# Trunk kernel on one core: who sums the two accumulators, in which order the first loads are requested, and when one weight panel is split

## The chip, the cores and the metric

One core of a Trainium2 chip runs the whole program. The metric is device time in microseconds (us), the median of several executions. The engines are TensorE (PE in the profile, its weight loads PEld), VectorE (DVE), ScalarE (ACT), GpSimd (POOL) and SyncE (SP), which here only requests transfers between HBM and the on-chip memory (SBUF).

## The reference, cut to what matters

Two layers of one trunk work on 256 context tokens and 512 latent tokens of width 1024, all in float32. The second layer drops the context tokens behind its keys and values, so most of its work is on 512 tokens.

```
for i in range(2):
    mod = silu(c) @ w_mod[i] + b_mod[i]           # six vectors per stream: sh1, sc1, gt1, sh2, sc2, gt2
    h = rmsnorm(x, g_mix[i]) * (1 + sc1) + sh1
    cq, ckv, kr, u, qs, ks, vs, gates = split(h @ w_in[i])
    y = merge(latent_attention(cq, ckv, kr), pooled(u), windowed_attention(qs, ks, vs), gates) @ w_out[i]
    x = x + gt1 * y
    f = rmsnorm(x, g_ffn[i]) * (1 + sc2) + sh2
    x = x + gt2 * (routed_experts(f, top 8 of 64) + shared_expert(f))
out = rmsnorm(x_latent, g_final)
```

## The kernel before, in words

**Jobs.** `make_plan` writes one list of jobs. TensorE runs all of them in that order. ScalarE and VectorE walk the same list, each doing its share (an eviction of PSUM, or extra work hung on the job). PSUM is divided into a few buffers used in rotation; `filled` counts jobs that TensorE has finished, `drained` counts evictions. The list begins with `cvec` (turns the two conditioning vectors), `vec 0` and `vec 1` (turn the small per-layer vectors of layer 0 and of layer 1: biases, gains), and then for panels 0 to 3 of the modulation of layer 0 the pair `modr` (16 matmuls on a 2 MB panel of `w_mod`, L933) and `mod` (8 small matmuls, L938). With panel 3 the scales are complete, and the eight `h` jobs turn the normalised tokens and apply scale and shift. Everything else of the layer follows from `h`.

**Loads at the start.** SP requests transfers in the order of its program (L642 to L724): constants, the conditioning vectors, `load_vectors(0)` (six small transfers), the tokens `ctx` (1 MB, L655) and `x` (2 MB, L656), modulation panel 0, `load_vectors(1)` (L650 again), modulation panels 1, 2 and 3, masks and tables. Weight panels go into a ring of three slots of 2 MB: panel n may be requested once the last job that reads panel n - 3 is filled (`load_panel`, L706). So modulation panel 3 is requested behind job `mod 0 0`. When the tokens have landed, ScalarE takes their sums of squares (six, L1237) ahead of its eviction of `modr 0 0`; VectorE then scales them (six, L1617) ahead of its part of `mod 0 0`, and behind its part of `vec 1`.

**Splitting of weights.** Some projections are computed from float32 operands split into a high and a low part: three matmuls each time (L832, L833, L834, in `project3`). ScalarE copies the high part of a piece (512 columns of the panel, `piece_high`), VectorE subtracts it from the piece (L1843, `piece_low`). The projection `u` of the pooled branch needs all eight of its pieces, numbers 12 to 19: `weights2` waits for `piece_low` 20. The order of jobs around it is `ks`, `vs`, `ksp`, `qs 0`, `qs 1`, `qsp 0`, `qs 2`, `qsp 1`, `qs 3`, `qsp 2`, `u 0`, `qsp 3`, `u 1` to `u 3`, and then the windowed attention. `qs` is a projection of 48 matmuls in layer 0 and 24 in layer 1, and `qsp` a small one (L1044) for the rotary part. `split_now` hangs the pieces on jobs: ScalarE splits behind its eviction of `qs n`, VectorE behind its work for `qsp n` (three instructions at L1443 to L1446 and two subtractions at L1689). Before, n is 1 for pieces 12 to 15 and 2 for pieces 16 to 19. The panel itself is requested when `vs` is filled.

**Behind the loop over experts.** The routed and shared results are gathered in HBM in two accumulators, since blocks of rows are added alternately to one and the other. When the loop of a layer is over, SP requests for each tile of 128 tokens both parts (512 KB each, L796). GpSimd adds them (L1990, semaphore `summed`), VectorE multiplies by gt2 (L1596) and adds the result to the tokens (L1597), ScalarE takes the sum of squares, and both work out the factor of the next norm (L1462, L1463 on VectorE). Layer 0 has six tiles and goes on to the `h` jobs of layer 1. Layer 1 has four tiles, each of which VectorE scales (L1590) and SP stores.

Of the kernel before, what the change touches and what calls it, by code (L numbers as in the profile page):

```python
# [13 lines left out]
ALU, ACT, AX = mybir.AluOpType, mybir.ActivationFunctionType, mybir.AxisListType  # L14

P = 128
# [3 lines left out]
NT, CT = TOK // P, CTX // P  # L20
# [34 lines left out]
def active(l):  # L55

    return list(range(NT)) if l < DEPTH - 1 else list(range(CT, NT))
# [239 lines left out]
def build(nc, x, c, ctx, c_ctx, w_mod, b_mod, g_mix, g_ffn, w_in, g_mla_q, g_mla_kv, w_mla_uq, w_mla_ukv, w_pool,  # L297
# [10 lines left out]
    with ExitStack() as stack:  # L308
# [3 lines left out]
        def sem(name):  # L312
            return stack.enter_context(nc.semaphore(name))
# [72 lines left out]
        XT = XA[:].rearrange("p (t d) -> p t d", t=NT)  # L386
# [62 lines left out]
        comb = [w[:, 2048 * i:2048 * i + 2048].rearrange("p (a n) -> p a n", a=2) for w in WSL[0:2] for i in range(3)]  # L449
# [14 lines left out]
        s_x, s_xs, s_xr = sem("s_x"), sem("s_xs"), sem("s_xr")  # L464
        s_csm, s_css = sem("s_csm"), sem("s_css")
        ssq_ready, var_ready, rstd_ready, xn_ready = sem("ssq_ready"), sem("var_ready"), sem("rstd_ready"), sem("xn_ready")
        pre_ssq, pre_var, pre_rstd, summed = sem("pre_ssq"), sem("pre_var"), sem("pre_rstd"), sem("summed")
        rms_rec, rms_sqrt, cn_ready = sem("rms_rec"), sem("rms_sqrt"), sem("cn_ready")
        roped, rope_copied = sem("roped"), sem("rope_copied")
        max_ready, exp_ready, rden_ready = sem("max_ready"), sem("exp_ready"), sem("rden_ready")  # L470
# [13 lines left out]
        s_comb, combined, s_out = [sem(f"s_comb{i}") for i in range(NT)], sem("combined"), sem("s_out")  # L484
# [17 lines left out]
        def after(eng, *name):  # L502

            j = names[name]
            eng.wait_ge(drained[j.drain], j.count)
# [11 lines left out]
        def attn(l, br, i):  # L517

            t, h = active(l)[i // HEADS], i % HEADS
            if br == "m":  # L520
                return t, h, 0, [(0, 0, 512), (512, 512, 256)] if t >= CT else [(0, 0, CTX)]
            if t < CT:
                return t, h, 512, [(512, 0, CTX)]
            a, b = max(CT, t - 1), min(NT - 1, t + 1)
            n = (b - a + 1) * P
            return t, h, 512 - n, [(512 - n, a * P, n), (512, 0, CTX)]
# [14 lines left out]
        def key_tiles(l, br, i):  # L541

            return [k // P + j for _, k, n in attn(l, br, i)[3] for j in range(n // P)]
# [17 lines left out]
        def norm_no(l, i):  # L561
            return [0, NT, 1 + NT + len(active(1))][l] + i + 1
# [45 lines left out]
        def split_now(kind, a):  # L608

            if kind == "S" and a[1] == "m" and 18 <= a[2] < 30:  # L610
                return [a[2] - 18]
            if kind in ("qs", "qsp"):
                return {1: [12, 13, 14, 15], 2: [16, 17, 18, 19]}.get(a[1], [])
            return []

        def gate_panel(l, n2, b):

            return DK // 2 * b + n2
# [4 lines left out]
        def gate_no(n2, b, cc):  # L623
            return DK * b + 2 * n2 + cc
# [16 lines left out]
        def _(sp):  # L641
# [4 lines left out]
            def load_vectors(l):  # L646
                at = 0
                for v in (b_mod, g_mix, g_ffn, pool_scale, g_mla_q, g_mla_kv):
                    rows = v.shape[1] // P
                    sp.dma_start(layer_vecs[l][at:at + rows, :], v[l].rearrange("(k p) -> k p", p=P)).then_inc(s_vecs[l], 16)  # L650
                    at += rows
                assert at == NVEC

            load_vectors(0)
            sp.dma_start(XT[:, 0:CT, :], ctx[0].rearrange("(t p) d -> p t d", p=P)).then_inc(s_x, 16)  # L655
            sp.dma_start(XT[:, CT:NT, :], x[0].rearrange("(t p) d -> p t d", p=P)).then_inc(s_x, 16)  # L656
            def kpn(w, a, b):
                return w[:, a:b].rearrange("(k p) n -> p k n", p=P)

# [38 lines left out]
            def load_panel(n):  # L698
                key, _ = panels[n]
                if n >= RING:  # L700

                    sp.wait_ge(filled, panels[n - RING][1].fill)
                for at, ks, src in panel_parts(key):
                    w = src.shape[2]
                    dst = ring[:, SLOT * (n % RING) + at:SLOT * (n % RING) + at + ks * w]
                    sp.dma_start(dst.rearrange("p (k n) -> p k n", k=ks), src).then_inc(s_panel[n % RING], 16)  # L706
# [3 lines left out]
            def load_until(key):  # L710
                while done[0] <= panel_no[key]:
                    load_panel(done[0])
                    done[0] += 1

            load_until(("mod", 0, 0))
            for l in range(1, DEPTH):
                load_vectors(l)
            load_until(("mod", 0, 3))
# [3 lines left out]
            for l in range(DEPTH):  # L722
                A = active(l)
# [443 lines left out]
        def _(act):  # L1167
# [60 lines left out]
            for job in act_jobs:  # L1228
# [192 lines left out]
                for i in split_now(kind, a) if kind != "qsp" else ():  # L1421
                    key, at, high = split_piece(l, i)
                    loaded(act, key)
                    if i == 4:

                        act.wait_ge(filled, panels[panel_no["qs_high", l] - RING][1].fill)
                    elif i == 12:
                        act.wait_ge(filled, names["yT", l, "m", NT - 1].fill)
                    copy(high, ring[:, at:at + 512]).then_inc(piece_high, 1)
# [3 lines left out]
        def _(dve):  # L1433
            vec = nc.vector
            tt, ts, stt = vec.tensor_tensor, vec.tensor_scalar, vec.scalar_tensor_tensor

            def link(ins):
                step("dve", dve, ins)
# [21 lines left out]
            def inv_mean(out_, in_, n):  # L1460

                link(ts(out_, in_, 1.0 / n, EPS, ALU.mult, ALU.add))  # L1462
                return vec.reciprocal(out_, out_)  # L1463
# [109 lines left out]
            def combine(l):  # L1573

                A = active(l)
                for s in range(2 if l < DEPTH - 1 else 1):
                    after(dve, "bc", l, "gt2", s)

                def finish(i):

                    t = A[i]
                    if l < DEPTH - 1:
                        dve.wait_ge(pre_ssq, NT * l + i + 1)
                        inv_mean(ssq[:, t:t + 1], ssq[:, t:t + 1], D).then_inc(pre_var, 1)
                        return
                    dve.wait_ge(ssq_ready, norm_no(l + 1, i))
                    inv_mean(ssq[:, t:t + 1], ssq[:, t:t + 1], D).then_inc(var_ready, 1)
                    dve.wait_ge(s_gfin, 16)
                    dve.wait_ge(rstd_ready, norm_no(l + 1, i))
                    stt(XT[:, t, :], XT[:, t, :], rstd[:, t:t + 1], BC["A2", 0], ALU.mult, ALU.mult)\  # L1590
                        .then_inc(fin_ready, 1)

                for i, t in enumerate(A):
                    a = comb[i]
                    dve.wait_ge(summed, i + 1 + (NT if l else 0))
                    link(tt(a[:, 0, :], a[:, 0, :], BC["gt2", 0 if t >= CT else 1], ALU.mult))  # L1596
                    tt(XT[:, t, :], XT[:, t, :], a[:, 0, :], ALU.add).then_inc(combined, 1)  # L1597
                    if i:
                        finish(i - 1)
                finish(len(A) - 1)  # L1600
# [6 lines left out]
            for job in jobs:  # L1607
                kind, a, ps = job.kind, job.args, slot[job.slot] if job.drain else None
                mine = job.drain == "dve"
                l = a[0] if a else 0  # L1610
# [23 lines left out]
                elif kind == "mod":  # L1634
# [6 lines left out]
                    if a[1] in (3, 11):  # L1641
# [4 lines left out]
                        i, g, m = (0, V_GM, 1) if a[1] == 3 else (1, V_GF, 4)  # L1646
# [12 lines left out]
                elif kind in ("rq", "rk"):  # L1659
                    i = int(kind == "rk")  # L1660
# [44 lines left out]
                elif kind == "S":  # L1705
                    _, br, i = a
                    t, h, at, parts = attn(l, br, i)
# [26 lines left out]
                elif kind == "PV":  # L1734
                    _, br, i = a
                    t, h = attn(l, br, i)[:2]
# [8 lines left out]
                elif kind == "yT":  # L1745
                    _, br, t = a
# [9 lines left out]
                elif kind == "b":  # L1756
                    _, n2, b, cc = a
                    i = gate_no(n2, b, cc)
# [9 lines left out]
                    i = gate_panel(*a[:3])  # L1768
# [4 lines left out]
                elif kind == "o":  # L1773
                    t = a[1]
# [65 lines left out]
                for i in split_now("S" if kind == "T" else kind, a) if kind == "qsp" or kind == "T" and a[3] == 0 else ():  # L1840
                    _, at, high = split_piece(l, i)
                    dve.wait_ge(piece_high, PIECES * l + i + 1)
                    tt(ring_r[:, at:at + 512], ring[:, at:at + 512], high, ALU.subtract).then_inc(piece_low, 1)  # L1843
# [3 lines left out]
        def _(pool):  # L1847
            gp = nc.gpsimd
# [22 lines left out]
            for l in range(DEPTH):  # L1871
                A, sl = active(l), L[l]
# [5 lines left out]
                for g in range(4):  # L1878
# [3 lines left out]
                    src, a, b = 0, lo + 1, hi  # L1882
                    for d in (1, 2, 4)[:g]:
                        a, b = a + d, b - d
# [99 lines left out]
                pool.sem_inc(turns, 1)  # L1984
                loop_end(pool)

                for i, t in enumerate(A):
                    a = comb[i]
                    pool.wait_ge(s_comb[i], 32 * (l + 1))
                    gp.tensor_tensor(a[:, 0, :], a[:, 0, :], a[:, 1, :], ALU.add).then_inc(summed, 1)  # L1990


def constants():

# [67 lines left out]
```

## Time and profile before

| | |
|---|---|
| median of 3 runs | 3455.66 us (3450.21 to 3458.8) |
| profiled execution | 3455.1 us, its span 3453.3 us |
| PE busy | 3139.9 us (91%) |
| DVE busy | 1740.1 us (50%) |
| ACT busy | 1369.1 us (40%) |
| POOL busy | 709.5 us (21%) |
| mean of HBM traffic | 222 GB/s |

The span is the time between the first and the last instruction of the profiled execution. A busy share is an average over very different stages. All times in rows are us from the start of the span, unless marked ns. The granted clock is 1.00 at 2.4 GHz and 0.50 at 1.2 GHz.

### The profile page before, as it was taken

The page shows a single profiled execution, that of the slowest core. Times are in us where ns is not written, and L with a number is a line of the kernel's source. Part 1 is how long each engine was busy: PE and PEld are TensorE (multiplying, and loading weights), DVE is VectorE, ACT ScalarE, POOL GpSimd, SP SyncE. Part 2 cuts the span into 40 slices and gives each one's busy share as a digit, 9 for nine tenths or more (in the row PEclk, how much of TensorE's full clock was granted, in tenths as well). Part 3 has the DMA queues.
Part 4 walks back from the last instruction along what each step waited for, and adds up shares of the span by engine and source line. Part 5 has one row for each costly group of instructions (what it writes and reads, how often), then busy time and mean ns, then how long its engine had stood idle before and what let it go on. Part 6 is the DMA issues. An engine that isn't in the chain of part 4 may idle for free.

```text
span 3453.3 us, 49036 instructions
## 1 busy us (share of the span) xinstructions
PE 3139.9 (91%) x14864; PEld 2221.4 (64%) x14864; DVE 1740.1 (50%) x2560; ACT 1369.1 (40%) x1977; POOL 709.5 (21%) x767
## 2 busy tenths in 40 slices
PE   6999999999997999999999499999996899999994
PEld 3468877899545666666666346776863666666663
DVE  1354371222354666666666336362333666666665
ACT  2253251221224555555554235252212555555552
POOL 0000310000062333323332200020003332333332
PEclk9999999999999999999999799999998899999997
DMA  6420113333328999999998510113232999999993
GB/s 225 120 86 7 52 44 104 128 128 134 138 67 323 343 355 343 348 351 354 351 345 278 167 50 1 34 56 92 92 118 98 338 345 334 338 343 336 326 329 129
DMA packets 223714, 703.54 MB, mean 204 GB/s; under 512 B 55650, under 2 KB 104196, under 8 KB 169428
## 3 DMA queue, kind: packets, MB, share of 16 engines
q1 hardware_dynamic: 176356, 601.80, 47.0%
q0 software_dynamic: 47248, 100.21, 10.9%
q8 instruction: 77, 1.26, 0.2%
q14 instruction: 33, 0.27, 0.0%
HBM read 669.89 MB, written 98.31 MB: 222 GB/s over the span
## 4 chain that ended last, share of the span: by engine, by line
PE 63%; DMA 19%; DVE 6%; issue 6%; ACT 3%; SPq 2%; another core or an unknown queue 1%; DVEq 1%; POOLq 0%; POOL 0%; ACTq 0%
DMA ring<-in_w_exp_up 9%; PE ps L825 7%; PE ps L906 6%; PE ps L832 6%; PE ps L833 6%; PE ps L834 6%; DMA region_v<-in_w_exp_up 5%; PE ps L854 5%; PE ps L1104 4%; PE ps L877 4%; DMA region_k<-in_w_exp_up 4%; PE ps L879 4%; PE ps L878 4%; PE ps L1009 3%; PE ps L1030 3%
## 5 line engine op out<-in xcount | busy, mean ns | idle before, releaser
L1956 POOL DMA_INDIRECT acc<-region_q,idx_out x141 | 226.3, 1605 | 922.3 <-DVE region_q L1569 815.3
L877 PE MATMUL ps<-region_h_split,region_q_split 128*128 128x512 f32 x846 | 349.8, 413 | 69.1 <-DVE region_q_split L1529 33.7
L1535 DVE TENSOR_TENSOR ring_split<-ring,region_h_split 128x1024 fp32r<-128x1024 f32 x210 | 246.8, 1222 | 252.5 <-ACT region_h_split L1171 242.4
L854 PEld LDWEIGHTS ps<-con,region_c 128*128 128x128 f32 x1686 | 220.2, 167 | 147.1 <-DVE region_c L1542 73.6
L1171 ACT ACTIVATE region_h_split<-ring 128x1024 fp32r<-128x1024 f32 x210 | 210.1, 1052 | 240.8 <-DMA ring<-in_w_exp_up 201.3
L834 PE MATMUL ps<-region_x_split,ring_split 128*128 128x384 f32 (+2 forms) x800 | 283.0, 354 | 0.0
L854 PE MATMUL ps<-con,region_c 128*128 128x128 f32 x1686 | 258.0, 281 | 26.2 <-DVE region_c L1542 18.0
L906 PE MATMUL ps<-ring,region_c 128*128 128x512 f32 x560 | 252.0, 593 | 1.0 <-DVE region_c L1547 1.0
L1171 ACT ACTIVATE region_q<-ps 128x512 f32<-128x512 f32 (+1 forms) x163 | 106.8, 655 | 351.2 <-PE ps L906 233.9
L877 PEld LDWEIGHTS ps<-region_h_split,region_q_split 128*128 128x128 f32 x846 | 162.0, 192 | 117.6 <-issue 88.0
L878 PE MATMUL ps<-ring_split,region_q_split 128*128 128x512 f32 x560 | 219.9, 393 | 0.0
L1349 ACT ACTIVATE region_c<-ps 128x768 f32<-128x768 f32 (+1 forms) x48 | 33.8, 704 | 410.1 <-PE ps L834 410.1
L1535 DVE TENSOR_TENSOR region_k_split<-region_k,region_h_split 128x1024 fp32r<-128x1024 f32 x108 | 127.0, 1222 | 137.5 <-ACT region_h_split L1171 126.5
L1535 DVE TENSOR_TENSOR region_v_split<-region_v,region_h_split 128x1024 fp32r<-128x1024 f32 x105 | 123.3, 1221 | 126.7 <-ACT region_h_split L1171 122.0
L1904 POOL DMA_DIRECT2D h_rows<-region_c x10 | 5.7, 572 | 818.3 <-DVE region_c L1793 818.3
L879 PE MATMUL ps<-region_h_split,region_c_split 128*128 128x512 f32 x426 | 168.9, 397 | 0.0
L906 PEld LDWEIGHTS ps<-ring,region_c 128*128 128x128 f32 x560 | 101.2, 190 | 101.8 <-issue 101.6
L879 PE MATMUL ps<-region_h_split,region_q_split 128*128 128x512 f32 x420 | 166.6, 397 | 0.0
L832 PE MATMUL ps<-region_x_split,region_q_split 128*128 128x384 f32 (+1 forms) x432 | 157.9, 365 | 7.5 <-DVE ring_split L1457 4.6
L1171 ACT ACTIVATE region_h_split<-region_k 128x1024 fp32r<-128x1024 f32 x108 | 108.4, 1053 | 129.0 <-DMA region_k<-in_w_exp_up 110.9
L834 PEld LDWEIGHTS ps<-region_x_split,ring_split 128*128 128x128 f32 x800 | 151.1, 189 | 11.7
L1171 ACT ACTIVATE region_h_split<-region_v 128x1024 fp32r<-128x1024 f32 x105 | 104.7, 1051 | 125.9 <-DMA region_v<-in_w_exp_up 103.5
(315 smaller groups left out, 6909.9 us busy)
## 6 DMA issues: line engine op xcount, KB each, us to landing
ring<-in_w_exp_gate SPq DMA_DIRECT2D x70, 1024.0 KB
ring<-in_w_exp_up SPq DMA_DIRECT2D x70, 1024.0 KB
ring<-in_w_exp_down SPq DMA_DIRECT2D x70, 1024.0 KB
ring<-in_w_mod SPq DMA_DIRECT2D x24, 2048.0 KB, 8.0
region_k<-in_w_exp_gate SPq DMA_DIRECT2D x36, 1024.0 KB
region_k<-in_w_exp_up SPq DMA_DIRECT2D x36, 1024.0 KB
region_k<-in_w_exp_down SPq DMA_DIRECT2D x36, 1024.0 KB
region_v<-in_w_exp_gate SPq DMA_DIRECT2D x35, 1024.0 KB
```

The lines of the kernel that those rows point to most:

```text
L825: last = mm(ps[0:rows, at:at + n], weight[k], src[k][:, tok:tok + n], start=k == 0, stop=k == len(weight) - 1)
L832: mm(o, wh, xh, start=k == 0, stop=False)
L833: mm(o, wh, xl, start=False, stop=False)
L834: last = mm(o, wl, xh, start=False, stop=k == len(stationary) - 1)
L854: last = nc.tensor.transpose(ps[0:t.shape[1], at:at + t.shape[0]], t, ident[0:t.shape[0], 0:t.shape[0]])
L877: mm(m_gu[s], xT_hi[s][:, k, :], high, start=k == 0, stop=False)
L878: mm(m_gu[s], xT_hi[s][:, k, :], low, start=False, stop=False)
L879: last = mm(m_gu[s], xT_lo[s][:, k, :], high, start=False, stop=k == DK - 1)
L906: last = mm(m_y[:, 512 * side:512 * side + 512], hTb[:, 1 - s, cc * P:cc * P + P], wdn[before][:, cc, 512 * side:512 * side + 512], start= ...
L1171: return A_(o, i, ACT.Copy)
L1535: tt(wgu_lo[w][:, :, 2 * c:2 * c + 2, :], wgu[w][:, :, 2 * c:2 * c + 2, :], wgu_hi[c], ALU.subtract).then_inc(sl["w_lo"], 1)
L1956: pool.indirect_dma_start(ACC[s], bass.IndirectOffsetOnAxis(ap=idx_out[:, s:s + 1], axis=0), yb[:, s, :], None, bounds_check=TOK - 1, oob_ ...
```

## The change

Three edits. VectorE takes over the sum of the two accumulators, waiting for the loads itself; the loop over tiles on GpSimd and its semaphore are gone. SP requests modulation panel 0 ahead of the tokens, and panel 1 ahead of the vectors of layer 1. Pieces 12 to 15 and 16 to 19 are split one job sooner, behind `qs 0` and `qs 1` on ScalarE and behind `qsp 0` and `qsp 1` on VectorE.

```diff
@@ split_now
             if kind in ("qs", "qsp"):
-                return {1: [12, 13, 14, 15], 2: [16, 17, 18, 19]}.get(a[1], [])
+                return {0: [12, 13, 14, 15], 1: [16, 17, 18, 19]}.get(a[1], [])
@@ SyncE
             load_vectors(0)
-            sp.dma_start(XT[:, 0:CT, :], ctx[0].rearrange("(t p) d -> p t d", p=P)).then_inc(s_x, 16)
-            sp.dma_start(XT[:, CT:NT, :], x[0].rearrange("(t p) d -> p t d", p=P)).then_inc(s_x, 16)
...
             load_until(("mod", 0, 0))
+            sp.dma_start(XT[:, 0:CT, :], ctx[0].rearrange("(t p) d -> p t d", p=P)).then_inc(s_x, 16)
+            sp.dma_start(XT[:, CT:NT, :], x[0].rearrange("(t p) d -> p t d", p=P)).then_inc(s_x, 16)
+            load_until(("mod", 0, 1))
             for l in range(1, DEPTH):
                 load_vectors(l)
             load_until(("mod", 0, 3))
@@ VectorE, combine
                 for i, t in enumerate(A):
                     a = comb[i]
-                    dve.wait_ge(summed, i + 1 + (NT if l else 0))
+                    dve.wait_ge(s_comb[i], 32 * (l + 1))
+                    link(tt(a[:, 0, :], a[:, 0, :], a[:, 1, :], ALU.add))
                     link(tt(a[:, 0, :], a[:, 0, :], BC["gt2", 0 if t >= CT else 1], ALU.mult))
                     tt(XT[:, t, :], XT[:, t, :], a[:, 0, :], ALU.add).then_inc(combined, 1)
@@ GpSimd, behind the loop
-                for i, t in enumerate(A):
-                    a = comb[i]
-                    pool.wait_ge(s_comb[i], 32 * (l + 1))
-                    gp.tensor_tensor(a[:, 0, :], a[:, 0, :], a[:, 1, :], ALU.add).then_inc(summed, 1)
```

## Rows read from the trace of the kernel before

**Rows 1.** TensorE's waits, 318 to 410 us and 2150 to 2230: total, times, longest.
```profile
PE ps L832 <- DVE ring_split L1843: 7.6, 1, 7.6
PE ps L832 <- DVE ring_split L1843: 7.0, 1, 7.0
```
**Rows 2.** Timeline of SP at the start: start us, us, instruction, count.
```profile
5.39 0.50 SPq L706 DMA_DIRECT2D ring<-in_w_mod  x1
...
27.23 0.37 SPq L706 DMA_DIRECT2D ring<-in_w_mod  x1
```
**Rows 3.** Chain that ended last, at the start: start us, us, what.
```profile
13.36 8.01 DMA region_k<-in_g_mla_kv
```
**Rows 4.** Transfers: size, us to landing (panel 0, panel 3, the `u` panel).
```profile
ring<-in_w_mod SPq DMA_DIRECT2D x1, 2048.0 KB, 15.1
ring<-in_w_mod SPq DMA_DIRECT2D x1, 2048.0 KB, 9.6
ring<-in_w_in SPq DMA_DIRECT2D x1, 2048.0 KB, 7.7
```
**Rows 5.** Timeline of PE and DVE at the start, idle time before in brackets.
```profile
21.72 3.64 PE L933 MATMUL ps<-ring,cT 128*32 128x512 f32 x16
...
22.99 4.07 DVE L1617 TENSOR_SCALAR region_q<-region_x,rstd 128x1024 f32<-128x1024 f32 x6 [0.62 <-ACT rstd L1240]
...
27.12 1.92 PE L933 MATMUL ps<-ring,cT 128*32 128x512 f32 x16
...
31.55 2.58 PE L933 MATMUL ps<-ring,cT 128*32 128x512 f32 x16 [0.67 <-DVE modT L1639]
...
36.95 3.64 PE L933 MATMUL ps<-ring,cT 128*32 128x512 f32 x16 [0.20 <-DVE modT L1639]
```
**Rows 6.** A stretch: busy PE, PEld, DVE, ACT, POOL, granted clock, DMA share, GB/s.
```profile
32.00:34.00 2.00, 2.00 (x16) 0.29 (x8) 0.00 (x0) 0.00 (x0) 0.00 (x0) 0.67 1.05 388
```
**Rows 7.** Chain that ended last around `u 0`, layer 0, then layer 1.
```profile
373.93 0.86 PE ps L1044 x2
...
383.11 0.87 PE ps L1044 x2
...
391.55 0.77 PE ps L832
...
401.51 0.86 PE ps L1044 x2
...
2229.18 0.77 PE ps L832
...
2237.27 0.86 PE ps L1044 x2
```
**Rows 8.** Timeline of DVE around `qsp 1`, layer 0, then layer 1.
```profile
379.75 2.50 DVE L1843 TENSOR_TENSOR ring_split<-ring,region_c_split 128x512 fp32r<-128x512 f32 x4
...
2215.82 0.69 DVE L1443 TENSOR_TENSOR region_c<-ps,region_v 128x512 f32<-128x512 f32 x1 [2.23 <-PE ps L1044]
...
2219.97 2.50 DVE L1843 TENSOR_TENSOR ring_split<-ring,region_c_split 128x512 fp32r<-128x512 f32 x4
```
**Rows 9.** Timeline behind the loop, layer 0.
```profile
1923.76 2.34 POOL L1990 TENSOR_TENSOR region_k<-region_k 128x1024 f32<-128x1024 f32 x1 [11.77 <-DMA region_k<-acc]
...
1927.49 3.24 DVE L1597 TENSOR_TENSOR region_x<-region_x,region_k 128x1024 f32<-128x1024 f32 x1
...
1952.31 0.15 DVE L1462 TENSOR_SCALAR ssq<-ssq 128x1 f32<-128x1 f32 x1
```
**Rows 10.** Timeline behind the loop, layer 1.
```profile
3424.42 2.33 POOL L1990 TENSOR_TENSOR region_k<-region_k 128x1024 f32<-128x1024 f32 x1 [15.11 <-DMA region_k<-acc]
...
3439.75 1.22 DVE L1596 TENSOR_TENSOR region_k<-region_k,region_q 128x1024 f32<-128x1024 f32 x1
...
3446.43 0.15 DVE L1462 TENSOR_SCALAR ssq<-ssq 128x1 f32<-128x1 f32 x1
```
**Rows 11.** The stretch of `u 0` in layer 1 at its clock.
```profile
2232.00:2234.00 2.00, 2.00 (x6) 1.53 (x5) 0.00 (x0) 0.00 (x0) 0.00 (x0) 0.50 0.00 0
```

More of the change, by code:

```diff
@@ L466, in build @@
         ssq_ready, var_ready, rstd_ready, xn_ready = sem("ssq_ready"), sem("var_ready"), sem("rstd_ready"), sem("xn_ready")
-        pre_ssq, pre_var, pre_rstd, summed = sem("pre_ssq"), sem("pre_var"), sem("pre_rstd"), sem("summed")
+        pre_ssq, pre_var, pre_rstd = sem("pre_ssq"), sem("pre_var"), sem("pre_rstd")
         rms_rec, rms_sqrt, cn_ready = sem("rms_rec"), sem("rms_sqrt"), sem("cn_ready")
```

## The prediction
> **What bounds the kernel now.** The page first: TensorE is busy for 91% of the span, so time is won where TensorE stands still and where nothing else can fill the hole. All three edits lie in such places, and the views to read are TensorE's waits, the timelines around the edits, and the transfers at the start.
>
> At the splits, the waits show one hole per layer: in layer 0 TensorE waits 7.6 us for VectorE's subtraction L1843, in layer 1 7.0 us [rows 1]. At the start the transfers bound: panel 0 lands 15.1 us behind its request at 5.39, so at 20.5, and job `modr 0 0` starts only at 21.72, when the last vector of layer 1 (requested at 13.36, 8.01 us on the way for 1 KB) has landed at 21.37 [rows 2 to 5]. Behind the loops TensorE has nothing to do; the chain runs from the first landed pair of tiles through GpSimd and VectorE, and VectorE's own chain is what ends last there [rows 9, 10].
>
> **Split of the pooled weights, layer 0.** No instruction is added; four copies on ScalarE and four subtractions on VectorE move one job ahead, twice. TensorE finishes `qsp 2` at 383.11 + 0.87 = 383.98 and starts `u 0` at 391.55 [rows 7]. In the changed kernel the last four subtractions run where the first four ran, at 379.75 for 2.50 us, done at 382.25 [rows 8], ahead of 383.98. So the hole closes: -7.6 us. ScalarE's first copies now wait for the panel. The `u` panel takes 7.7 us to land [rows 4]; it is requested when `vs` is filled, and one `qs` (8.3 us: from 373.93 + 0.86 to 383.11 [rows 7]) and `ksp` lie between that and the first copy. It is there in time.
>
> The hole also costs clock. `u 0` takes from 391.55 to 401.51, 9.96 us, and the `qs` with as many matmuls of the same sizes 8.32 us [rows 7]: the difference is the stretch behind the hole at the lower level (1.2 GHz), shown as 0.50 in layer 1 [rows 11]. With no hole I count it as gained: -1.6 us. If the clock drops all the same, this term is 0.
>
> **Layer 1.** Here `qs` is shorter (two thirds of 8.32 is 5.5 us), so things are tighter. VectorE's work for `qsp 1` starts at 2215.82 and the subtractions behind it at 2219.97, 4.15 us later [rows 8]. Now four subtractions (2.50) stand ahead of it too, behind the work for `qsp 0`, which (TensorE's `qs` being 5.5 + 0.9 = 6.4 us apart) ends near 2215.82 - 6.4 + 4.15 = 2213.6. They end at 2216.1, 0.3 late. Then 4.15 and 2.50 us: all eight pieces are ready at 2222.7, and `u 0` starts near 2222.9 in place of 2229.18 [rows 7]: -6.3 us, 0.7 of the 7.0 being left. ScalarE has the panel 7.7 us after the request and `qs 0` evicted after about 6.4 us, so its first copies start 1 us or so late and end before `qs 1` is evicted. `u 0` took 2237.27 - 2229.18 = 8.1 us and would take 5.5 at the full clock [rows 7]: -2.6 us, none if the clock falls.
>
> What is late next: `qsp 3` and the stacked queries and keys for the windowed attention, which hide behind `u 1` to `u 3` (16 us or more) and move with `u 0`.
>
> **The sum behind the loop, layer 0.** Removed: six additions on GpSimd, the first of which takes 2.34 us, and six hand-overs. Added: six additions on VectorE, of two SBUF inputs and 1024 columns like L1596, which takes 1.22 us when GpSimd is idle [rows 10]. Beside GpSimd's additions VectorE's L1597, of the same size, takes 3.24 us [rows 9]; that goes away with them. VectorE's chain is then 3 x 1.22 = 3.66 us a tile and, from the second tile on, some 0.3 us of small instructions (0.15 us each [rows 9]). From 1923.76, when the first pair has landed, to the end of the sixth addition: 6 x 3.66 + 4 x 0.3 = 23.2, so 1946.9, against 1952.31 (the small instruction right behind that addition [rows 9]): -5.4 us. Pairs landed at least as fast as GpSimd took them, one in 2.6 to 3.3 us, so none is late for a tile each 3.9 us. ScalarE needs about 2.8 us a tile and stays hidden.
>
> **Layer 1.** Four tiles. From 3439.75 to 3446.43 VectorE does two tiles of two instructions (4 x 1.22 = 4.9) and one final norm, which so takes 1.8 us, the wait for ScalarE included [rows 10]. New: 3424.42 + 4 x 3.66 + 2 x 1.8 = 3442.7, against 3446.43: -3.7 us. The tail behind it (last norm, last store) is the same. The bound on the other side for both layers: if the additions took 3.24 us as the slow ones do, see the rivals.
>
> **The loads at the start.** The edit changes no byte, only order. The list of jobs still has `vec 1` ahead of `modr 0 0`, and `load_vectors(1)` now stands behind panel 1 as well as behind panel 0 and the tokens. The queue delivers in order as far as the rows show: the last vector, 1 KB, came 0.9 us behind panel 0 although it was requested at 13.36 [rows 3, 4]. One panel more ahead of it is 2.1 MB at the 388 GB/s seen in this stage [rows 6], 5.4 us. So `vec 1`, and with it `modr 0 0`, moves from 21.7 to 27.1: panel 0, asked for first, lands early and lies there. Behind that, panel 1 and mostly panel 2 have landed, so the later waits go: 0.67 us ahead of the third `modr` and up to 0.20 ahead of the fourth [rows 5]. Panel 3 is requested when `mod 0 0` is filled, at 27.23 before and at 32.7 now, when the queue has run nearly empty; it lands like the lone `u` panel, 7.7 us later [rows 4], at 40.4, and is wanted at about 36.95 + 4.6 = 41.5: just in time. So +5.4 - 0.7 - 0.1 = +4.6 us up to the `h` jobs.
>
> The tokens land one panel later, near 20.5, as panel 0 did. ScalarE's squares and VectorE's scaling (22.99 for 4.07, behind `vec 1` [rows 5]) move by the same 5.4 and stay beside `modr 0 0`. Masks, tables and the `ckv` panel come later too, but the latter had over 10 us to spare. Bounds of this term: the four `modr` need 3.64, 1.92, 2.58 and 3.64 us [rows 5], the long ones being at the lower clock (0.67 and falling at 32 us [rows 6]). Were the last two at 1.92, 3.6 us of the 4.6 would come back, and panel 3's landing allows no more: +1.0. At the slow level in all of them it would be +6.3. I take +4.6, since the same work with smaller holes starts from the same idle engine.
>
> A rule bears on this. The Trainium skill, "DMA: Bandwidth & Descriptors", section "Queues, rings and completion order", says that each DMA engine consumes the descriptors of a ring in order, and that a completion signal comes only behind all earlier writes of that engine. By it the small vectors can't pass panel 1, and the term is the +4.6; if they could pass, it would be zero. The trace agrees, with 8.01 us for 1 KB.
>
> **The sum.** -7.6 - 1.6 - 6.3 - 2.6 - 5.4 - 3.7 + 4.6 = -22.6 us. The profiled execution took 3455.1 us, 1.8 outside its span, and the median is 3455.66, so: 3433 us. Between the places, TensorE works almost without a hole, and the loops over experts start when their table is ready, so a shift passes through.
>
> **The rivals.** (a) The start costs nothing, since the small vectors pass panel 1 or TensorE doesn't need them as argued: -27.2, 3428 us. For it: they are tiny and touch few DMA engines. Against: the 8.01 us [rows 3].
>
> (b) The holes at the splits close, but something else waits in their place: ScalarE held up by the panel, or a later wait in attention or merging that takes the gain back. Then the 18.1 us of the split go wholly or in part: -4.5 us at the least, 3451; by half, 3442. For it: layer 1 is tight by under 1 us. Against: nothing but TensorE's own work stands behind `u 0` for 16 us and more.
>
> (c) VectorE's slow instructions behind the loop are slow from the transfers that write into SBUF at the time, not from GpSimd. Then its 30 instructions take 3.24 us each: layer 0 is 18 x 3.24 + 1.2 = 59.5 against 28.6 before, layer 1 12 x 3.24 + 3.6 = 42.5 against 22.0, together +51.4; with the other terms +37.9, 3493 us. It decides from 2.0 us per instruction up: 30 x (1.22 + 0.75) eats the 22.6. Against it: L1596 at 1.22 and the chain's last tiles; in the stretch after the loads had ended, VectorE was still slow as long as GpSimd added.
>
> (d) `split_now` is read by both engines for the same job index, so that both halves really move; that the edit does nothing is under 1%, and part of (b).
>
> **Chances.** The sum 0.75, (a) 0.09, (b) 0.12, (c) and anything else that ends slower 0.04. The likeliest one's own range is 3427 to 3439: the clock terms may be 0 (+4.2), the start between +1.0 and +6.3, and medians of this kernel scatter by a few us. The range is 3424 to 3445, which takes in (a) and the halved (b). A change of 0.3% (10 us, below 3445.3 or above 3466) is about what a measurement of this kernel can tell. Faster: 0.75 + 0.09 + half of (b) = 0.90 less a little for terms not seen, 0.88. Same: 0.08. Slower: 0.04.
>
> **What the profile would show.** Right: no wait on L1843 in layer 0 and under 1 us in layer 1, clock 1.00 through `u 0`; L1596 and L1597 at 1.22 us in all tiles and no GpSimd there; the first `modr` near 27 us and the first `h` some 4.6 us later than 43. Wrong: the first `modr` at 22 us or before (then (a)); a new wait of ScalarE on the `u` panel that delays an eviction (b); additions of 3 us with GpSimd idle (c).

## The result and the profile after

The changed kernel takes 3434.04 us (median of 4 runs, 3430.36 to 3439.47) against 3455.1 us for the kernel before (4 runs), ratio 0.9941 with a 95% interval of 0.9925 to 0.9956. Two later groups of runs gave 0.9962 (0.9949 to 0.9975) and 0.9955 (0.9940 to 0.9970). The mean of the three is 0.9953, some 16 us. So it is faster, clear of the scatter in all three, but by 16 us and not by the 22.6 of the forecast; only the first group, with 21, comes near it.

The executions of one kernel differ by up to 25 us here (3430.4 to 3455.0 in the third group of the changed kernel), more than any term of the sum. A single run can't test a term of 4 us; a stage of the trace can. The reading below therefore goes by stages, each measured between two fixed instructions. Line numbers of the changed kernel are 1 or 2 higher than those before (L833 was L832, L934 was L933, L1845 was L1843, L1599 was L1597).

**The split.** Waits in layer 1, 2200 to 2260 us (ScalarE's for the panel, TensorE's for the subtraction; in layer 0 no wait on the split is left), answering [rows 1]:

```profile
ACT region_c_split L1172 <- DMA ring<-in_w_in: 0.8, 1, 0.8
...
PE ps L833 <- DVE ring_split L1845: 0.7, 1, 0.7
```

The chain that ended last around `u 0` of layer 0, start us and us, answering [rows 7]:

```profile
377.84 0.86 PE ps L1045 x2
...
387.02 0.86 PE ps L1045 x2
...
396.24 0.86 PE ps L1045 x2
```

VectorE's timeline around `qsp 1` of layer 1, answering [rows 8]:

```profile
2212.87 2.50 DVE L1845 TENSOR_TENSOR ring_split<-ring,region_c_split 128x512 fp32r<-128x512 f32 x4
2215.29 0.69 DVE L1444 TENSOR_TENSOR region_c<-ps,region_v 128x512 f32<-128x512 f32 x1
...
2219.44 2.50 DVE L1845 TENSOR_TENSOR ring_split<-ring,region_v_split 128x512 fp32r<-128x512 f32 x4
```

And the stretches around `u 0` in both layers (busy PE, PEld, DVE, ACT, POOL, granted clock, DMA share, GB/s), answering [rows 11]:

```profile
388.00:392.00 4.00, 4.00 (x19) 3.30 (x18) 3.02 (x5) 1.69 (x2) 0.00 (x0) 1.00 0.93 313
...
2222.00:2226.00 4.00, 3.92 (x17) 3.30 (x18) 3.20 (x5) 1.26 (x2) 0.00 (x0) 1.00 0.19 58
```

`u 0` starts right behind `qsp 2` at 387.88 and ends 8.36 us later; before, 17.5 us passed between the same two points [rows 7]. The whole 7.6 us are gone and the clock stays at 1.00. In layer 1 the second group of subtractions ends at 2221.9, and 0.7 us of waiting are left, as worked out. ScalarE waits 0.8 us for the panel there (forecast: its copies start 1 us or so late), and delays nothing by it.

**The sum.** The timeline behind the loop of layer 0, ScalarE's evictions of gt2 included, answering [rows 9]:

```profile
1925.32 1.02 ACT L1172 ACTIVATE region_q<-ps 128x1024 f32<-128x1024 f32 x1 [13.40 <-PE ps L1096]
1927.62 1.02 ACT L1172 ACTIVATE region_q<-ps 128x1024 f32<-128x1024 f32 x1 [1.27 <-PE ps L1096]
1928.73 1.23 DVE L1597 TENSOR_TENSOR region_k<-region_k 128x1024 f32<-128x1024 f32 x1 [16.69 <-ACT region_q L1172]
1929.99 1.23 DVE L1598 TENSOR_TENSOR region_k<-region_k,region_q 128x1024 f32<-128x1024 f32 x1
1931.25 1.23 DVE L1599 TENSOR_TENSOR region_x<-region_x,region_k 128x1024 f32<-128x1024 f32 x1
...
1951.66 0.15 DVE L1463 TENSOR_SCALAR ssq<-ssq 128x1 f32<-128x1 f32 x1
```

and of layer 1, answering [rows 10]:

```profile
3412.39 1.23 DVE L1597 TENSOR_TENSOR region_k<-region_k 128x1024 f32<-128x1024 f32 x1 [17.57 <-DMA region_k<-acc]
...
3430.79 0.15 DVE L1463 TENSOR_SCALAR ssq<-ssq 128x1 f32<-128x1 f32 x1
```

Every addition and multiplication takes 1.2 us. Layer 1's chain takes 18.4 us from its first addition (forecast 18.3). Layer 0's takes 22.9 (forecast 23.2), but look at the bracket of the first addition: its releaser is not a transfer but ScalarE, which has just evicted gt2. VectorE's additions stand behind its wait for that broadcast; GpSimd's did not.

**The start.** SP, ScalarE and TensorE in the changed kernel, answering [rows 2, 5]:

```profile
6.00 1.82 SPq L704 DMA_DIRECT2D ring<-in_w_mod  x1
...
7.87 9.15 SPq L650 DMA_DIRECT2D region_k<-in_b_mod  x1
...
18.41 0.25 SPq L650 DMA_DIRECT2D region_k<-in_g_mla_kv  x1
...
20.40 1.06 ACT L1238 ACTIVATE region_h<-region_x 128x1024 f32<-128x1024 f32 x1 [14.98 <-DMA region_x<-in_x]
...
26.65 0.38 PE L855 MATMUL ps<-con,region_k 73*128 73x73 f32 x1 [19.30 <-DMA region_k<-in_g_mla_kv]
...
26.96 3.64 PE L934 MATMUL ps<-ring,cT 128*32 128x512 f32 x16
...
33.18 3.64 PE L934 MATMUL ps<-ring,cT 128*32 128x512 f32 x16
...
39.39 3.23 PE L934 MATMUL ps<-ring,cT 128*32 128x512 f32 x16
...
44.39 1.92 PE L934 MATMUL ps<-ring,cT 128*32 128x512 f32 x16
...
48.19 0.17 DVE L1641 TENSOR_TENSOR modT<-ps,vecT 128x8 f32<-128x8 f32 x1 [3.52 <-PE ps L939]
```

And a stretch of the same (columns as above), answering [rows 6]:

```profile
32.00:34.00 2.00, 2.00 (x10) 1.37 (x14) 0.53 (x2) 0.00 (x0) 0.00 (x0) 1.00 0.00 0
```

`vec 1` (L855) waits for the last vector of layer 1 until 26.65, and `modr 0 0` starts at 26.96, against 21.72 [rows 5]. The transfers now pause: at 32 to 34 us nothing moves (before: 388 GB/s [rows 6]), since panel 3 may be requested only when `mod 0 0` is filled. The granted clock of this row is no evidence: the trace of this execution has no clock record ahead of 42.1 us, and the view then shows 1.00, while the three `modr` up to there took 3.64, 3.64 and 3.23 us. The fourth `mod` is evicted at 48.19; in the kernel before it was at 43.3.

### The profile page after: what moved, and what is told of

Read it like the earlier page. It is cut to its first block, busy times and chain, and to the rows that moved or that the text cites. A ratio compares the mean times of both kernels' runs of the same rounds, so it can differ in the third digit from the quotient of the medians.

```text
span 3437.7 us, 49036 instructions
## 1 busy us (share of the span) xinstructions
PE 3139.2 (91%) x14864; PEld 2222.2 (65%) x14864; DVE 1734.8 (50%) x2570; ACT 1369.1 (40%) x1977; POOL 676.9 (20%) x757
## 3 DMA queue, kind: packets, MB, share of 16 engines
q1 hardware_dynamic: 176356, 601.80, 47.2%
## 4 chain that ended last, share of the span: by engine, by line
PE 61%; DMA 20%; issue 8%; DVE 6%; ACT 2%; SPq 2%; DVEq 1%; POOLq 0%; ACTq 0%; POOL 0%
DMA ring<-in_w_exp_up 8%; PE ps L826 7%; DMA region_v<-in_w_exp_up 6%; PE ps L907 6%; PE ps L833 6%; PE ps L834 6%; PE ps L835 6%; PE ps L855 5%; DMA region_k<-in_w_exp_up 4%; PE ps L1105 4%; PE ps L878 4%; PE ps L880 3%; PE ps L879 3%; PE ps L1010 3%; PE ps L1031 3%
## 5 line engine op out<-in xcount | busy, mean ns | idle before, releaser
L1958 POOL DMA_INDIRECT acc<-region_q,idx_out x141 | 226.3, 1605 | 925.0 <-DVE region_q L1570 816.7
L855 PEld LDWEIGHTS ps<-con,region_c 128*128 128x128 f32 x1686 | 221.2, 167 | 145.9 <-DVE region_c L1543 74.3
L855 PE MATMUL ps<-con,region_c 128*128 128x128 f32 x1686 | 258.9, 282 | 25.9 <-DVE region_c L1543 17.5
L833 PE MATMUL ps<-region_x_split,region_q_split 128*128 128x384 f32 (+1 forms) x432 | 159.1, 368 | 7.5 <-DVE ring_split L1458 4.6
```

Source lines behind the costliest of these rows:

```text
L833: mm(o, wh, xh, start=k == 0, stop=False)
L855: last = nc.tensor.transpose(ps[0:t.shape[1], at:at + t.shape[0]], t, ident[0:t.shape[0], 0:t.shape[0]])
L1958: pool.indirect_dma_start(ACC[s], bass.IndirectOffsetOnAxis(ap=idx_out[:, s:s + 1], axis=0), yb[:, s, :], None, bounds_check=TOK - 1, oob_ ...
```

## The experiments

Eleven runs in three groups (e1 to e4, e5 to e8, e9 to e11), each group beside runs of the kernel before. All were changed from the kernel after, unless the text says otherwise. A ratio is against the kernel before, with its 95% interval.

**e1_no_start**: the old order of the first loads, the two other edits kept.
```diff
-            load_until(("mod", 0, 0))
             sp.dma_start(XT[:, 0:CT, :], ctx[0]...)
             sp.dma_start(XT[:, CT:NT, :], x[0]...)
-            load_until(("mod", 0, 1))
+            load_until(("mod", 0, 0))
```


> The changed kernel with the old order of the first loads (tokens, panel 0, vectors of layer 1). Theory (the sum of the prediction): the new order costs 4 to 5 us, so this one is faster than the changed kernel, about 27 us below the kernel before (ratio 0.992), with the first modr at 21.7 us, the end of the fourth mod job at 43.2 and the clock falling to 0.50 between 33 and 46 us as before. Rival (the start is free, since what is behind it waits for something else, or the lost time comes back in a later stage): the same time as the changed kernel, 21 us below the kernel before.

Measured: 0.9944 (0.9929 to 0.9959), 20 us below the kernel before and not 27 (its 0.992 lies outside the interval); fourth `mod` at 40.6 us. The two last `modr`:
```profile
33.01 1.92 PE L933 MATMUL ps<-ring,cT 128*32 128x512 f32 x16
...
36.84 1.92 PE L933 MATMUL ps<-ring,cT 128*32 128x512 f32 x16
```
The fourth starts when its panel lands, as before, but here the granted clock is 1.00 and the stage ended 2.6 us sooner than in the profile of before, where it was 0.50 at the fourth `modr`. My expectation that the clock would fall as before was wrong. It differs between executions of one kernel: in the changed kernel it stays at 1.00 from 42 us on, in the same kernel as e5 it is 0.50 there.

**e2_only_split**: from the kernel before, the line of `split_now` alone.
```diff
-                return {1: [12, 13, 14, 15], 2: [16, 17, 18, 19]}.get(a[1], [])
+                return {0: [12, 13, 14, 15], 1: [16, 17, 18, 19]}.get(a[1], [])
```


> The kernel before with the earlier split alone. Theory: 7.6 + 1.6 us in layer 0 and 6.3 + 2.6 in layer 1, together 18 us (ratio 0.9948); u 0 takes 8.4 us in layer 0 and 5.5 in layer 1, with the clock at 1.00. Rival (the wait goes but the time is given back in a later wait or by the clock): the holes close in the trace and the time falls by less than 10 us.

Measured: 0.9954 (0.9938 to 0.9970), 16 us where 18 were expected. The stages close as in the changed kernel: 8.2 us for `u 0` in layer 0; in layer 1 the same wait of 0.7 us, and 31.8 us from `ksp` to `qsp 3` against 40.4 to 40.6 in the three kernels with the late split. The time of the whole program falls with them by 16 of 18 us, so nothing later gives them back beyond the scatter. The theory holds.

**e3_only_sum**: from the kernel before, the sum on VectorE alone.
```diff
-                    dve.wait_ge(summed, i + 1 + (NT if l else 0))
+                    dve.wait_ge(s_comb[i], 32 * (l + 1))
+                    link(tt(a[:, 0, :], a[:, 0, :], a[:, 1, :], ALU.add))
```
(and GpSimd's loop of additions gone.)

> The kernel before with VectorE's sum alone. Theory: 5.4 + 3.7 = 9 us (ratio 0.9974): each tile takes 3.9 us on VectorE in layer 0, all its instructions 1.22 us. Rival (the transfers and not GpSimd make VectorE's instructions slow): they stay at 3.2 us wherever loads are under way, and the kernel is no faster or slower.

Measured: 0.9986 (0.9977 to 0.9995), 5 us. The instructions of which some took 3.24 us before, minimum, median and maximum in ns:
```profile
L1598 DVE TENSOR_TENSOR region_x<-region_x,region_k x6: 1224/1224/1226, 1934.8 to 3430.3; 128x1024 f32<-128x1024 f32 x6
```
None is slow, under the same loads: it was GpSimd. But the gain is short of 9 us, and the stage tells where: from the last scattered block to the small instruction (L1462) right behind the last addition, 38.5 us in layer 0 against 41.9, and 35.2 in layer 1 against 38.7. Layer 1 has its 3.5; layer 0 has 3.4 in place of 5.4.

**e4_only_start**: from the kernel before, the new order of the loads alone.
```diff
+            load_until(("mod", 0, 0))
             sp.dma_start(XT[:, 0:CT, :], ctx[0]...)
             sp.dma_start(XT[:, CT:NT, :], x[0]...)
-            load_until(("mod", 0, 0))
+            load_until(("mod", 0, 1))
```


> The kernel before with the new order of the first loads alone. Theory: 4 to 5 us slower (ratio 1.0013), the first modr at 27.0 us, the end of the fourth mod job 4.9 us later than before, 1 us of that regained in the h jobs, which find the clock at its full level. Rival (start is free): no difference from the kernel before.

Measured: 1.0020 (1.0009 to 1.0030), 7 us slower, first `modr` at 27.10, fourth `mod` at 48.4. By itself this edit is a loss, clear of noise, and rather more than the 4 to 5 us expected. The rival (a) of the prediction falls.

**e5_after_again**, the changed kernel unchanged.

> The changed kernel unchanged, for a second profile and times beside the other experiments. Its first profiled span was 15.6 us below that of the kernel before, while the sum of its stages gave 22 and the medians 21. Theory: the missing 6 us were lost by chance in the stage between the router and the loop over experts of layer 0, which differs between executions of one kernel; here that stage (from the projection u 0 of layer 0 to the first scattered block) is shorter again. Rival: that stage is longer in the changed kernel for good, by 5 us or more, as a result of the change.

Measured: 0.9962. The stage in question took 136.3 us, the longest of all; the first profile of the changed kernel had 130.5 and that of before 124.4. The theory that it would be shorter here was wrong, and chance isn't proved by it either; e11 comes back to it. At the start the fourth `modr` now waits for its panel (the bracket names the evicted `mod`, but that was over at 39.82):
```profile
40.52 3.04 PE L934 MATMUL ps<-ring,cT 128*32 128x512 f32 x16 [0.90 <-DVE modT L1641]
```
Panel 3, requested at 32.3 us, takes 8.2 us and lands at 40.4, as forecast.

**e6_later**: one panel more ahead of the vectors.
```diff
-            load_until(("mod", 0, 1))
+            load_until(("mod", 0, 2))
```


> The changed kernel with the vectors of layer 1 requested behind panel 2 as well (one more panel of 2 MB ahead of them). Theory (TensorE's second job waits for these vectors and for nothing else): the first modr starts at 32.4 us, 5.4 later, and the four pairs follow without a hole; about 5 us slower than the changed kernel, 16 below the kernel before. Rival (the start waits for the tokens and ScalarE's squares, not for the vectors): no change from the changed kernel.

Measured: 0.9968 (0.9957 to 0.9979), 1 us above the changed kernel beside it (e5), where 5 were expected; times of whole programs can't tell the two.
```profile
31.92 3.19 PE L934 MATMUL ps<-ring,cT 128*32 128x512 f32 x16
...
45.03 3.46 PE L934 MATMUL ps<-ring,cT 128*32 128x512 f32 x16 [0.70 <-DVE modT L1641]
```
The first `modr` moves by another 5.0 us with one panel more: 21.7, 27.0, 31.9. That is the dose that the theory asks for. The fourth `mod` ends at 50.4, 2 to 4 us behind the changed kernel and not 5, since the four pairs took 18.4 us here, with two of the `modr` at 1.92 us, against 19.1 to 21.2 in the changed kernel.

**e7_early_new** and **e8_early_old**: the vectors of layer 1 requested behind `load_vectors(0)`, with panel 0 ahead of the tokens (e7) or behind them (e8).
```diff
             load_vectors(0)
...
+            for l in range(1, DEPTH):
+                load_vectors(l)
```
(and not behind the panels.)

> The changed kernel with the vectors of layer 1 requested ahead of panel 0, the rest in the new order. Theory: modr 0 0 starts when panel 0 has landed, near 12 us, but its eviction stands behind ScalarE's squares of the tokens, which land at 20.5, so near 28.3; the third copy of the chain from there: the fourth mod job ends near 46, some 2 us before the changed kernel and 3 behind the kernel before. Rival (the vectors alone cost the 5 us): it ends at 43 or before.

> The two other edits with the tokens first, as in the kernel before, but the vectors of layer 1 ahead of the tokens. Theory: modr 0 0 starts with panel 0 at about 21, modr 0 1 and 0 2 with their panels at 27 and 31.5, and panel 3 lands at 37 whatever the order, since the transfers are the limit up to there: the same as the old order, 27 to 28 us below the kernel before. Rival (the vectors' wait costs in the kernel before too): 1 us or more faster still than the old order.

Measured: e7 0.9958 (0.9940 to 0.9976), e8 0.9943 (0.9921 to 0.9964). In e7, TensorE and ScalarE:
```profile
14.39 3.64 PE L934 MATMUL ps<-ring,cT 128*32 128x512 f32 x16 [6.11 <-issue]
29.77 0.58 ACT L1172 ACTIVATE ring<-ps 128x512 f32<-128x512 f32 x1
30.50 1.84 PE L939 MATMUL ps<-con,ring 128*128 128x2 f32 x8 [12.47 <-ACT ring L1172]
```
`modr 0 0` now runs at 14.39, and TensorE then stands still for 12.5 us: its eviction stands in ScalarE's program behind the six squares of tokens that have landed a panel later. So the wait for the vectors is only the first of two waits that the new order lengthens. I had the mechanism but not the size: fourth `mod` at 49.9 in place of 46, since the eviction came at 29.8 and not 28.3 (the tokens landed at 22.0 and not 20.5) and three of the four `modr` took 3.64 us. e8 has the fourth `mod` at 43.6, no better than the old order: there the panels' landing is the limit (panel 3 lands at 38.14, the fourth `modr` starts at 38.23). Its time is 18 us below the kernel before, not 27 to 28.

**e9_best**: e1 with the first tile's sum ahead of the wait for gt2.
```diff
+                dve.wait_ge(s_comb[0], 32 * (l + 1))
+                link(tt(comb[0][:, 0, :], comb[0][:, 0, :], comb[0][:, 1, :], ALU.add))
                 for s in range(2 if l < DEPTH - 1 else 1):
                     after(dve, "bc", l, "gt2", s)
```
(and the loop's own sum only for the tiles behind the first.)

> Old order of the first loads, earlier split, VectorE's sum, and the sum of the first tile moved ahead of VectorE's wait for the broadcast gt2. In the changed kernel VectorE's first addition in layer 0 starts 15.8 us behind the last scattered block, when ScalarE has evicted gt2 (the pair of tiles had landed about 13.3 us behind it). Theory (that wait is what the stage lost against the forecast): the first addition starts near 13.3 us behind the last scatter and ends before gt2 is there, the stage is 1.2 us shorter than in the changed kernel (37.5 in place of 38.7 to 39.4), layer 1 is unchanged at 35.1; the time is 1 us below the one without it, which the clock of a whole run can't tell. Rival (the pair lands later in the changed kernel): the first addition starts at 15.8 all the same.

Measured: 0.9942 (0.9923 to 0.9961).
```profile
1920.55 1.22 DVE L1577 TENSOR_TENSOR region_k<-region_k 128x1024 f32<-128x1024 f32 x1 [14.25 <-DMA region_k<-acc]
1923.74 1.23 DVE L1600 TENSOR_TENSOR region_k<-region_k,region_q 128x1024 f32<-128x1024 f32 x1 [1.97 <-ACT region_q L1171]
```
The last block was scattered at 1907.2, so the pair is there 13.3 us later, as it was for GpSimd, and the rest of the wait is for gt2: that is the loss. The stage took 38.2 us. How long it takes without the move hangs on when gt2 is there: in e9 and e5 ScalarE has evicted it 16.4 us behind the last scatter, and beside e5's 39.4 the move saves the 1.2 us expected; in the first profile of the changed kernel gt2 came at 15.7, and the stage took 38.7. No time of a whole run shows it.

**e10_no_start_again** and **e11_after_third**: e1 and the changed kernel, side by side on one chip.

> The changed kernel with the old order of the first loads, again, beside the changed kernel on the same chip. Theory: 5 to 8 us faster than the changed kernel; the fourth mod job ends between 40.6 and 43.3 us (its panel lands at 36.9, and the clock of the four modr differs between executions), against 46 to 48. Rival (no cost at the start): within 2 us of it.

> The changed kernel a third time, on the same chip as the two others. Theory: 0.994 to 0.996 of the kernel before, the fourth mod job at 46 to 48.4 us; the stage from the request of the shared down projection to the first scattered block anywhere between 124 and 136 us, as in all kernels so far. Rival: that stage is 130 us or more whenever the start is in the new order.

Measured: e10 0.9947 (0.9930 to 0.9964), fourth `mod` at 43.2; e11 0.9955 (0.9940 to 0.9970), fourth `mod` at 46.2, the doubtful stage 131.3 us. The old order is ahead by 3 us at this measurement, inside both intervals: neither the 5 to 8 us of the theory nor the rival's 2 us or less. e11's rival (the doubtful stage takes 130 us or more whenever the start is in the new order) holds here, and e4 comes to 129.8 us.

The stages of all profiles, in us, worked out from the times of instructions. 4th `mod` is the start of VectorE's part of it; `u 0` goes from the end of `qsp 2` to the start of `qsp 3`; the next stage from the request of the shared down projection to the first block that GpSimd scatters, behind the router; loop 0 from there to the last block; behind a loop, from the last block to the L1462 right behind the last addition.

| | 4th `mod` | `u 0`, layer 0 | shared weights to first scatter | loop 0 | behind loop 0 | `ksp` to `qsp 3`, layer 1 | behind loop 1 |
|---|---|---|---|---|---|---|---|
| before | 43.3 | 17.4 | 124.4 | 816.5 | 41.9 | 40.5 | 38.7 |
| after | 48.2 | 8.2 | 130.5 | 816.7 | 38.7 | 31.8 | 35.1 |
| e5 (after) | 46.2 | 8.2 | 136.3 | 816.1 | 39.4 | 31.8 | 35.2 |
| e11 (after) | 46.2 | 8.2 | 131.3 | 817.0 | 38.3 | 31.8 | 35.2 |
| e1 old order | 40.6 | 8.2 | 126.2 | 815.9 | 38.9 | 31.7 | 35.1 |
| e10 old order | 43.2 | 8.2 | 129.9 | 816.9 | 38.5 | 31.8 | 35.2 |
| e9 old order | 43.0 | 8.2 | 127.3 | 818.4 | 38.2 | 31.8 | 35.1 |
| e8 old order | 43.6 | 8.2 | 131.7 | 815.8 | 39.0 | 31.8 | 35.5 |
| e2 split alone | 40.8 | 8.2 | 129.9 | 817.1 | 41.9 | 31.8 | 38.7 |
| e3 sum alone | 40.8 | 18.4 | 129.9 | 816.9 | 38.5 | 40.4 | 35.2 |
| e4 start alone | 48.4 | 18.4 | 129.8 | 816.0 | 42.0 | 40.6 | 38.9 |
| e6 one panel more | 50.4 | 8.2 | 131.5 | 817.7 | 38.1 | 31.8 | 35.2 |
| e7 vectors early | 49.9 | 8.2 | 134.2 | 816.6 | 38.7 | 31.8 | 35.5 |

## Why the prediction was right, and where not

**The split: right in mechanism and size.** -9.2 us in layer 0 (17.4 to 8.2) as forecast, -8.7 in layer 1 (40.5 to 31.8) against -8.9. The clock terms, which I counted in full, came in full. They are not one size: behind the same hole of 7.6 us, `u 0` took 1.0 us longer still in e3 and e4 (18.4 in place of 17.4). Rival (b) falls with e2.

**The sum in layer 1: right**, -3.6 against -3.7. VectorE's slow instructions were GpSimd's doing, and rival (c) falls with e3.

**The sum in layer 0: mis-sized**, -3.2 us in the pair of profiles (41.9 to 38.7) against -5.4. The step that failed is "From 1923.76, when the first pair has landed": I let VectorE's first addition start where GpSimd's had, and did not ask what else stands ahead of it in VectorE's program. It is the wait for the broadcast of gt2. GpSimd added in its shadow; VectorE begins 15.8 us behind the last scatter, not 13.3. e9 shows the two waits apart. In layer 1 the first pair is there only 16.7 us behind the last scatter (g_final is requested ahead of it) and gt2, of one stream only, after 14.6, so nothing is lost there.

**The start: right in size, and for the wait that I named**, 5.2 us more until the first `modr` (forecast 5.4) and +4.9 us at the fourth `mod` (forecast +4.6). Over all profiles, 41.9 in the mean with the old order (43.3, 40.6, 40.8, 40.8, 43.2, 43.0) and 47.2 with the new (48.2, 48.4, 46.2, 46.2): +5.3. The bounds of that term covered it. That the pair of profiles gave 4.9 for 4.6 is in part luck. I took over the four `modr` of before, and they came out otherwise: 3.64, 3.64, 3.23 and 1.92 us for 3.64, 1.92, 2.58 and 3.64, and 2.9 us at the fourth `mod` in e5 and e11. Nor do the rows bear out that all the long ones were at the lower clock: the fourth was (the row below, of the kernel before), but the first of them, at 21.72, lies ahead of the first clock record of its trace (25.9 us).

```profile
38.00:40.00 2.00, 2.00 (x15) 0.23 (x6) 0.00 (x0) 0.00 (x0) 0.00 (x0) 0.50 0.93 373
```

What I had not seen is that the squares of the tokens are a second wait of nearly the same length (e7).

**The sum of it.** In the pair of profiles: +4.9, -1.0 for the `h` jobs, which met the full clock, -9.2, -8.7, -3.2, -3.6: -20.8 us. The two spans differ by only 15.6. The changed kernel loses 6.1 us in the stage from the shared weights to the first scattered block and 1.6 ahead of it, and gains 2.5 in later stages. That stage takes 124 to 136 us in these profiles. With the old order it is 124.4, 126.2, 127.3, 129.9 (three times) and 131.7, with the new 129.8, 130.5, 131.3 and 136.3, and 131.5 and 134.2 in e6 and e7. That is 128.5 in the mean against 132.3, and e4's 7 us, of which the start explains 4, point the same way. It may be that the new order costs some us there too; but the ranges overlap, no step of the change lies in it, and its own runs differ by 6. It stays open. So the forecast of 3433 was met within 1 us by the first four runs with luck: the three groups together give 16 us, the accounted terms 21. The kernels with the old order show that the gap isn't the start's alone: for them the forecast was 27 us, their stages account for 25, and the times of the four (e1, e8, e9, e10) lie 18 to 20 us below the kernel before. Where those 5 us go is not shown; the 124.4 of the kernel before is the lowest value of the doubtful stage, and from one profile.

Of the versions tried, those with the old order (e1, e10, e9, e8: 0.9942 to 0.9947) lie 0.0006 to 0.0011 ahead of the changed kernel's mean of 0.9953, which is less than one interval; the direct test (e4) shows the loss clearly.

## What to carry to other kernels

When an instruction moves to another engine, read what stands ahead of it in that engine's program, not only what its data waits for: here a wait that the old engine never had took 2.4 us of the gain. A request moved forward in a queue pushes everything behind it, and the smallest transfer behind it may be the one that the first job waits for; count the jobs' order, not the bytes. And when an execution scatters by more than a term, measure the term between two fixed instructions of the trace.

## What the runs showed of the hardware

**The clock of TensorE after short holes is not the same twice.** In the merging stage of layer 0 every kernel has the same wait of 2.0 us. The stretch behind it, in the kernel before, in the changed one, and in the changed one again (e5; columns as above):

```profile
552.00:556.00 4.00, 3.65 (x21) 3.65 (x22) 0.37 (x2) 0.00 (x0) 0.00 (x0) 1.00 0.97 367
```
```profile
548.00:552.00 4.00, 4.00 (x17) 4.00 (x17) 0.00 (x0) 0.00 (x0) 0.00 (x0) 0.67 1.05 403
```
```profile
547.00:551.00 4.00, 4.00 (x25) 4.00 (x24) 0.00 (x0) 0.00 (x0) 0.00 (x0) 1.00 1.05 402
```
Same hole, same work, yet once the clock stays and once it falls. From the end of the hole to ScalarE's next instruction it takes 8.6 to 8.7 us in six profiles, where the clock stayed at 1.00, and 10.2 us in the seven others, where it fell: 1.6 us lost. At the start the changed kernel's second `modr` took 3.64 us in one execution and 1.92 in e5, but there no clock record tells the level. The edit that removes a hole gains the clock behind it; one that leaves the hole in place may gain or lose 1.6 us by luck.

**GpSimd and VectorE take turns.** GpSimd's addition takes 2.34 us alone; while both add, GpSimd's takes 3.3 us (two in 6.62, the row below, of the kernel before) and VectorE's 3.24 in place of 1.22 [rows 9, 10], so each seems to wait out the other's instruction.

```profile
1926.32 6.62 POOL L1990 TENSOR_TENSOR region_k<-region_k 128x1024 f32<-128x1024 f32 x2 [0.22 <-DMA region_k<-acc]
```

The loads are not needed for it: from 1940 to 1944 us in the kernel before nothing moves (0 GB/s), and VectorE's addition at 1940.63 beside GpSimd's still takes 3.25 us. This is the rule of the Trainium skill, "SBUF — State Buffer", section "SBUF: two separate sides": the port pair that the two share is an exclusive lock held for a whole instruction, when VectorE's has two inputs in SBUF and GpSimd's reads SBUF. The traces agree: 1.20 to 1.23 us for all 30 instructions once GpSimd is silent, under loads of about 400 GB/s.

**A request can block its queue.** In the changed kernel SP's request of panel 1 took 1.82 us and that of 24 KB behind it 9.15, with 7 MB requested ahead of it. The request of the last vector of layer 1 stands behind it in SP's program: it went out at 13.36 us in the kernel before, at 18.42 in e5 and at 23.56 in e6, and the vector landed 8.0 us behind its own request each time (8.2 in the first profile of the changed kernel, request at 18.41). So the time that a panel costs the vectors shows as a request held back in SP, not as a longer way. Whether they would have landed sooner without the block isn't shown.
